# Delta-rule heads: the q/k norm of the next head ahead of this head's output, the second weight unit split in two steps, a new order in the prologue

## The chip, the cores and the metric

The kernel runs on one core of one Trainium2 chip. A core has four engines that matter here and run side by side: PE (TensorE, matrix multiplies), DVE (VectorE), ACT (ScalarE) and POOL (GpSimd). SP issues the weight transfers. Each engine works through its own list of instructions in the order in which they are written; they meet only at semaphores. The metric is the device time of one execution in microseconds (us), as the median of several runs.

## What is computed

Three layers on a 256 x 2048 activation in float32: a first block and two hybrid attention layers. The change touches the gated delta-rule part of the first block only. Cut to what matters there:

```python
h = rmsnorm(x, norm1_w[l])
proj = h @ w_in[l]
u_pool, q, k, v, z, a, bt, xr, gr = jnp.split(proj, cuts, axis=-1)
...
y_gdn = gated_deltanet(q, k, v, z, a, bt, gdn_conv_w[l], gdn_a_log[l], gdn_dt_bias[l], gdn_norm_w[l])
...
def l2norm(t):
    return t * lax.rsqrt(jnp.sum(t * t, axis=-1, keepdims=True) + EPS)
```

Six heads of 128 columns (`GH`). For each, q, k and v go through a causal convolution of four taps and a silu, q and k through `l2norm`, and then through the gated delta rule in chunks of 64 tokens: decays from cumulated gates, the inverse of a triangular matrix, a state handed from chunk to chunk. The output is normalised and multiplied by silu(z).

## The kernel before

**Weights.** Every weight matrix arrives in units of 128 x 2048 floats in the four buffers of `raw`. A float32 product is made of three passes with rounded halves: ACT copies `raw` to `w_hi` (L161), DVE subtracts to get `w_lo` (L166), each in two parts of 768 and 1280 columns, and PE runs three matmuls a tile (L197 to L199 in this stage): `w_hi` with the high and the low half of the activation, `w_lo` with the high half. A unit is 16 tiles, so 48 matmuls.

**Two kinds of work on PE.** In the delta-rule stage PE mixes the small matmuls of a head (`mix` of the tensor block, its variable j) with the projection of the next head's q, k, v and z. The function `fill(n)` issues n pieces of two tiles (six matmuls) of that projection; a head holds 32 pieces, four units numbered (i, 0) to (i, 3). Piece 3 of each unit is the first that needs the second part of `w_lo`. So PE has always something to do between two small steps, as long as what the small step waits for is ready when the pieces ahead of it are done.

**One head on PE**, in order: the sum of squares of q and k (`qk_ss`, one matmul pair of 512 columns); two pieces; the gate rows (`grow`, from `gb`, into `m[2]`); two pieces; a wait for `k_t`, the normalised k (`k_normed`); the transposes of k and v and the products k·k and k·q (`kkq`); five pieces; a wait for `u1`, that is for `tu` written at the end of DVE's chain; then five levels of the inverse, the state steps, the output, and its norm, with 21 more pieces among them.

**One head on DVE and ACT.** Their `mix(j, side)` holds the steps of head j, and `side(k)` calls put the steps of the next head's projection, convolution and silu between them. The order of both is written out by hand; nothing else sets it. Five of the six heads are one rolled loop (`Fori(1, GH)`), the last is written out behind it with `pool_side`. At the start of head j, ACT makes the norm factor from `qk_ss` (Ln, then Exp into `rs`), splits unit (i, 1) as a whole, finishes the silu of z of the head before (`sigmoid(i - 1, 3)`), makes `expg` from `grow`, and then the exponential of `dec`. DVE makes `q_t` and `k_t` from `rs`, one step of that silu (`one_plus`), the two `w_lo` parts of unit (i, 1), then `dec` from `grow` (it also waits for `expg`), waits for ACT's exponential (`edec`), and goes on through `dd`, `aa`, `xm` to `tu` (`u1`). At the end of a head come the output `oy` (DVE), its product with silu(z) on POOL (`oz`), the copy of its high half to `mixed` (ACT, `mix_hi`), the low half (DVE, `mix_lo`), `take(i, 3)` (DVE, the scaled z of the next head out of PSUM) and `take_z(i)` (ACT).

**The prologue** projects head 0, computes the gates (`gate_logs`, `beta`, `sums`, `bexpg`, `egd`) in a chain of tiny DVE operations, splits unit (1, 0) and squares q and k of head 0 (`squares(0)` into `sq`).

## Time and profile before

| | us |
|---|---|
| median of 3 runs (3514.66 to 3526.53) | 3518.19 |
| the profiled execution, its own time | 3525.01 |
| its span | 3523.3 |
| PE busy | 3413.3 (97%) |
| DVE busy | 2160.6 (61%) |
| ACT busy | 1701.2 (48%) |
| granted TensorE clock, mean | 0.991 |

The delta-rule heads take the stretch from 55 to about 322 us of the span. How to read it: PE is the engine that nearly always works, so time is what PE does plus what PE waits. The rows in the section after the next show single instructions with their start, their busy time, and in brackets the idle time of that engine just before and what ended it.

### The profile page before, as it was taken

The page shows a single profiled execution, that of the slowest core. Times are in us where ns is not written, and L with a number is a line of the kernel's source. Part 1 is how long each engine was busy: PE and PEld are TensorE (multiplying, and loading weights), DVE is VectorE, ACT ScalarE, POOL GpSimd, SP SyncE. Part 2 cuts the span into 40 slices and gives each one's busy share as a digit, 9 for nine tenths or more (in the row PEclk, how much of TensorE's full clock was granted, in tenths as well). Part 3 has the DMA queues.
Part 4 walks back from the last instruction along what each step waited for, and adds up shares of the span by engine and source line. Part 5 has one row for each costly group of instructions (what it writes and reads, how often), then busy time and mean ns, then how long its engine had stood idle before and what let it go on. Part 6 is the DMA issues. An engine that isn't in the chain of part 4 may idle for free. (4 is left out here: it accounts for less than half of the span.)

```text
span 3523.3 us, 73388 instructions
## 1 busy us (share of the span) xinstructions
PE 3413.3 (97%) x28014; PEld 3336.7 (95%) x28014; DVE 2160.6 (61%) x3526; ACT 1701.2 (48%) x2776; POOL 182.6 (5%) x208
## 2 busy tenths in 40 slices
PE   7889699999999999999999999999999999999999
PEld 7888699999999998899999999999899999999999
DVE  6666556656656665667755565555567765566554
ACT  4443544434434454655544554444565554554443
POOL 1000010000000014000000000000000000000000
PEclk9999899999999999999999999999999999999999
DMA  4223355555555554334455445454334355445554
GB/s 176 95 95 111 114 181 178 189 191 179 188 189 182 181 190 166 132 144 155 146 179 203 169 163 184 181 191 176 135 144 155 137 180 200 174 151 180 189 191 167
DMA packets 90613, 584.18 MB, mean 166 GB/s; under 512 B 10481, under 2 KB 11121, under 8 KB 28401
## 3 DMA queue, kind: packets, MB, share of 16 engines
q1 hardware_dynamic: 88992, 577.60, 46.4%
q0 software_dynamic: 1488, 4.72, 0.4%
q8 instruction: 94, 1.54, 0.2%
q14 instruction: 39, 0.31, 0.0%
HBM read 580.19 MB, written 2.10 MB: 165 GB/s over the span
## 5 line engine op out<-in xcount | busy, mean ns | idle before, releaser
L185 PE MATMUL bank<-h,w_hi 128*128 128x256 f32 x5808 | 1658.9, 286 | 37.7 <-DVE w_lo L166 28.2
L166 DVE TENSOR_TENSOR w_lo<-raw,w_hi 128x768 fp32r<-128x768 f32 (+5 forms) x1202 | 1347.8, 1130 | 471.0 <-ACT w_hi L161 468.0
L186 PE MATMUL bank<-h,w_hi 128*128 128x256 f32 x5808 | 1628.1, 280 | 0.0
L187 PE MATMUL bank<-h,w_lo 128*128 128x256 f32 x5808 | 1623.4, 280 | 0.0
L161 ACT ACTIVATE w_hi<-raw 128x768 fp32r<-128x768 f32 (+5 forms) x1202 | 1106.0, 968 | 253.6 <-PE bank L187 232.1
L185 PEld LDWEIGHTS bank<-h,w_hi 128*128 128x128 f32 x5808 | 1096.4, 189 | 53.3 <-issue 26.1
L186 PEld LDWEIGHTS bank<-h,w_hi 128*128 128x128 f32 x5808 | 1097.6, 189 | 2.8 <-issue 1.4
L187 PEld LDWEIGHTS bank<-h,w_lo 128*128 128x128 f32 x5808 | 1096.9, 189 | 0.0
L185 PE MATMUL bank<-mixed,w_hi 128*128 128x256 f32 x2400 | 677.1, 282 | 25.3 <-DVE mixed L990 15.9
L186 PE MATMUL bank<-mixed,w_hi 128*128 128x256 f32 x2400 | 673.3, 281 | 0.0
L187 PE MATMUL bank<-mixed,w_lo 128*128 128x256 f32 x2400 | 671.3, 280 | 0.0
L185 PEld LDWEIGHTS bank<-mixed,w_hi 128*128 128x128 f32 x2400 | 453.8, 189 | 26.9 <-DVE mixed L990 16.3
L186 PEld LDWEIGHTS bank<-mixed,w_hi 128*128 128x128 f32 x2400 | 454.2, 189 | 0.2
L187 PEld LDWEIGHTS bank<-mixed,w_lo 128*128 128x128 f32 x2400 | 453.9, 189 | 0.0
L222 DVE TENSOR_TENSOR pre<-bank,rn 128x256 f32<-128x256 f32 x246 | 103.9, 422 | 127.2 <-PE bank L187 126.7
L1781 ACT ACTIVATE sgy<-sgy 128x256 f32<-128x256 f32 x64 | 26.7, 418 | 291.0 <-DVE sgy L222 291.0
L222 DVE TENSOR_TENSOR sgy<-bank,rn 128x256 f32<-128x256 f32 x96 | 40.8, 425 | 194.3 <-PE bank L187 194.3
L197 PE MATMUL bank<-h,w_hi 128*128 128x256 f32 x432 | 137.7, 319 | 0.0
L1627 ACT ACTIVATE sqx<-pre 128x256 f32<-128x256 f32 x80 | 32.4, 414 | 192.2 <-DVE pre L222 192.2
L198 PE MATMUL bank<-h,w_hi 128*128 128x256 f32 x432 | 122.3, 283 | 0.0
L199 PE MATMUL bank<-h,w_lo 128*128 128x256 f32 x432 | 122.0, 282 | 0.0
L1580 POOL TENSOR_TENSOR zs<-pre,sig 128x256 f32<-128x256 f32 x48 | 39.8, 834 | 1311.9 <-DVE oy L1915 856.1
(351 smaller groups left out, 2574.4 us busy)
## 6 DMA issues: line engine op xcount, KB each, us to landing
raw<-in_w SPq DMA_DIRECT2D x485, 1024.0 KB, 4.8
raw<-in_w_br SPq DMA_DIRECT2D x96, 512.0 KB, 4.3
raw<-in_w_uq SPq DMA_DIRECT2D x8, 768.0 KB, 4.2
raw<-in_w_ukv SPq DMA_DIRECT2D x8, 512.0 KB, 3.3
bias_t<-in_bias POOLq DMA_DIRECT2D x16, 192.0 KB, 3.2
x<-in_x SPq DMA_DIRECT2D x4, 512.0 KB, 8.5
raw<-in_w_kr SPq DMA_DIRECT2D x4, 512.0 KB, 3.2
out_x<-x SPq DMA_DIRECT2D x3, 512.0 KB, 7.6
```

Of the source, the lines that this page charges most:

```text
L161: act.activation(w_hi[:, b % 2, c], raw[:, b, c], ACT.Copy).then_inc(S["hi_done"], 1)
L166: dve.tensor_tensor(w_lo[:, b % 2, c], raw[:, b, c], w_hi[:, b % 2, c].bitcast(F32), ALU.subtract).then_inc(S["lo_done"], 1)
L185: pe.matmul(o, w_hi[:, b % 2, c], a_hi, start=start and k == t0, stop=False)
L186: pe.matmul(o, w_hi[:, b % 2, c], a_lo, start=False, stop=False)
L187: last = pe.matmul(o, w_lo[:, b % 2, c], a_hi, start=False, stop=stop and k == t0 + nt - 1)
L197: pe.matmul(o, w_hi[:, b % 2, c], a_hi, start=k == 0, stop=False)
L198: pe.matmul(o, w_hi[:, b % 2, c], a_lo, start=False, stop=False)
L199: last = pe.matmul(o, w_lo[:, b % 2, c], a_hi, start=False, stop=k == KT - 1)
L222: return dve.tensor_tensor(dst, src[:, 0:SEQ], rn[:, :], ALU.mult)
L1580: pool.tensor_tensor(zs[:, e, :], pre[:, 7 + e, :], sig[:, e, :], ALU.mult).then_inc(S["z_silu"], 1)
L1627: act.activation(sq[:, k, :], src, ACT.Square).then_inc(S["h_sq"], 1)
L1781: act.activation(sg[:, b // 2, :], sg[:, b // 2, :], ACT.Sigmoid).then_inc(S["gate_sig"], 1)
```

## The change

On ACT, the two steps that make the norm factor of head j+1 (`norm_factor(j + 1)`) move from the start of the next head to this head's end, between `side(3)` and the wait for `oz`; `expg` of head j+1 (`decay_rows(j + 1)`) moves behind the copy to `mixed` and ahead of `take_z`. On DVE, `q_t` and `k_t` of head j+1 (`qk_normed(j + 1)`) move ahead of the wait for `mix_hi`. The split of unit (i, 1) comes in two steps. ACT: first part ahead of the exponential of `dec`, second part behind it. DVE: `dec` first, then `one_plus` and the first part, and the second part behind `qdec`, after `u1`.

In the prologue, ACT squares q and k of head 0 and splits unit (1, 0) ahead of the convolution of v; DVE makes the gate columns between the two parts of unit (1, 0), and `q_t` and `k_t` of head 0 ahead of the last gate steps. PE waits once more, for `sums_sb`, ahead of the transposes of k. PE's order of instructions is the same.

```diff
+        def split_hi_part(act, n, b, k, cols=UNIT):
+            at_least(act, f"raw_full{b}", 16 * n + 16)
+            at_least(act, "unit_done", 4 * n + b - 1)
+            c = parts(cols)[k]
+            act.activation(w_hi[:, b % 2, c], raw[:, b, c], ACT.Copy).then_inc(S["hi_done"], 1)
...
                 def side(k):
-                    if k == 0:
-                        split_hi(act, i, 1)
+                    if k == "split":
+                        split_hi_part(act, i, 1, 0)
+                    elif k == 0:
+                        split_hi_part(act, i, 1, 1)
                         sigmoid(i - 1, 3)
...
-            def mix(j, side):
+            def norm_factor(j):
                 act.wait_ge(S["qk_ss"], j + 1)
...
-                side(0)
+
+            def decay_rows(j):
                 act.wait_ge(S["grow"], j + 1)
                 act.activation(expg[:, :], m[2][:, 0:SEQ], ACT.Exp).then_inc(S["expg"], 1)
+
+            def mix(j, side, more=True):
+                side("split")
                 act.wait_ge(S["dec"], 2 * j + 2)
                 act.activation(dec[:, :], dec[:, :], ACT.Exp).then_inc(S["edec"], 1)
+                side(0)
...
                 side(3)
+                if more:
+                    norm_factor(j + 1)
                 act.wait_ge(S["oz"], j + 1)
...
+                if more:
+                    decay_rows(j + 1)
                 side(4)
...
-            split_hi(act, 1, 0)
-            squares(0)
+                    squares(0)
+                    split_hi(act, 1, 0)
+            norm_factor(0)
+            decay_rows(0)
             take_z(0)
...
                     if k == 0:
                         one_plus(i - 1, 3)
-                        split_lo(dve, i, 1)
+                        split_lo_part(dve, i, 1, 0)
+                    elif k == "split":
+                        split_lo_part(dve, i, 1, 1)
...
-            def mix(j, side):
+            def qk_normed(j):
                 dve.wait_ge(S["qk_rs"], j + 1)
...
-                side(0)
+
+            def mix(j, side, more=True):
                 dve.wait_ge(S["grow"], j + 1)
...
                                       gcum[:, p, bass.ds(j, 1)], 0.0, ALU.subtract, ALU.min).then_inc(S["dec"], 1)
+                side(0)
                 dve.wait_ge(S["edec"], j + 1)
...
                 dve.tensor_tensor(qdec[:, :], q_t[:, :], expg[:, :], ALU.mult).then_inc(S["qdec"], 1)
+                side("split")
                 side(1)
...
                 side(13)
+                if more:
+                    qk_normed(j + 1)
                 dve.wait_ge(S["mix_hi"], j + 1)
...
-            split_lo(dve, 1, 0)
-            take(0, 3)
-
+            split_lo_part(dve, 1, 0, 0)
             dve.wait_ge(S["beta_e"], 1)
...
+            dve.wait_ge(S["gate_g"], 1)
+            gate_columns(0)
+            split_lo_part(dve, 1, 0, 1)
+            take(0, 3)
             dve.wait_ge(S["gate_sums"], 1)
             dve.tensor_copy(sums[:, :], m[1][:, 32:60]).then_inc(S["sums_sb"], 1)
+            qk_normed(0)
...
-            gate_columns(0)
...
                 pe.wait_ge(S["k_normed"], j + 1)
                 pe.wait_ge(S["silu"], 4 * j + 3)
+                pe.wait_ge(S["sums_sb"], 1)
```

DVE at the end of the loop's body and behind the branch; `COMPARE_AND_BRANCH` closes an iteration, and `k_t` is what PE waits for early in a head. Before:

```order
L874 ISA [waits mix_hi]
L874 REGISTER_ALU
L874 TENSOR_TENSOR mixed<-oy,mixed 128x256
L690 REGISTER_ALU
L222 TENSOR_TENSOR pre<-bank,rn 128x256 [waits silu,unit_done]
L947 REGISTER_ALU
L947 COMPARE_AND_BRANCH
L812 SCALAR_TENSOR_TENSOR q_t<-pre,rs 128x256 [waits qk_rs]
L813 TENSOR_TENSOR k_t<-pre,rs 128x256
L707 TENSOR_SCALAR sig<-sig 128x256 [waits silu_e]
L166 TENSOR_TENSOR w_lo<-raw,w_hi 128x768 [waits hi_done]
L166 TENSOR_TENSOR w_lo<-raw,w_hi 128x1280 [waits hi_done]
```

The same place of the changed kernel:

```order
L837 SCALAR_TENSOR_TENSOR q_t<-pre,rs 128x256 [waits qk_rs]
L838 TENSOR_TENSOR k_t<-pre,rs 128x256
L904 ISA [waits mix_hi]
L904 REGISTER_ALU
L904 TENSOR_TENSOR mixed<-oy,mixed 128x256
L711 REGISTER_ALU
L228 TENSOR_TENSOR pre<-bank,rn 128x256 [waits silu,unit_done]
L979 REGISTER_ALU
L979 COMPARE_AND_BRANCH
L845 TENSOR_SCALAR dec<-m,gcum 128x128 [waits expg,grow]
```

`q_t` and `k_t` now stand ahead of the branch and of the low half of the output, and `dec` is the first operation behind the branch.

ACT at the start of a head. Before:

```order
L508 ACTIVATE rs<-m,eps 128x512 [waits qk_ss]
L511 ACTIVATE rs<-rs 128x512 [waits qk_ln]
L161 ACTIVATE w_hi<-raw 128x768 [waits unit_done,raw_full1]
L161 ACTIVATE w_hi<-raw 128x1280
L448 ACTIVATE sig<-sig 128x256 [waits silu_1p]
L450 ACTIVATE sig<-sig 128x256 [waits silu_ln]
L514 ACTIVATE expg<-m 128x256 [waits grow]
L516 ACTIVATE dec<-dec 128x256 [waits dec]
```

The same place of the changed kernel:

```order
L167 ACTIVATE w_hi<-raw 128x768 [waits unit_done,raw_full1]
L530 ACTIVATE dec<-dec 128x256 [waits dec]
L167 ACTIVATE w_hi<-raw 128x1280 [waits unit_done,raw_full1]
L454 ACTIVATE sig<-sig 128x256 [waits silu_1p]
L456 ACTIVATE sig<-sig 128x256 [waits silu_ln]
```

The factor and `expg` are gone from here (they stand at the end of the head before), and one part of the split is left ahead of the exponential of `dec`.

## Rows read from the trace of the kernel before

**Rows 1.** The page's first section: busy time and share of each engine.
```profile
PE 3413.3 (97%) x28014; PEld 3336.7 (95%) x28014; DVE 2160.6 (61%) x3526; ACT 1701.2 (48%) x2776; POOL 182.6 (5%) x208
```

**Rows 2.** The waits of PE, whole span: total us, times, longest us.
```profile
PE m L1092 <- DVE k_t L813: 11.9, 5, 2.4
PE m L1120 <- ACT sq L471: 5.0, 5, 4.2
...
PE m L1092 <- DVE tu L836: 2.8, 3, 0.9
```

**Rows 3.** Timeline, PE, head 2: start, us, instruction, [idle before, what ended it].
```profile
143.30 1.12 PE L1120 MATMUL m<-sq,shared 128*128 128x512 f32 x2 [0.21 <-ACT sq L471]
...
146.10 0.61 PE L1127 MATMUL m<-shared,gb 128*128 128x128 f32 x4
...
150.50 0.41 PE L1092 MATMUL m<-shared,k_t 128*128 128x128 f32 x2 [2.38 <-DVE k_t L813]
...
156.47 0.44 PE L1092 MATMUL m<-shared,tu 128*128 128x128 f32 x2 [0.95 <-DVE tu L836]
```

**Rows 4.** Timeline, ACT, the same head.
```profile
144.28 0.42 ACT L450 ACTIVATE sig<-sig 128x256 f32<-128x256 f32 x1
...
147.81 0.42 ACT L461 ACTIVATE sig<-pre 128x256 f32<-128x256 f32 x1 [1.05 <-DVE pre L222]
148.13 0.67 ACT L508 ACTIVATE rs<-m,eps 128x512 f32<-128x512 f32 x1
148.83 0.63 ACT L511 ACTIVATE rs<-rs 128x512 f32<-128x512 f32 x1
```

**Rows 5.** Timeline, DVE, the same head.
```profile
147.36 0.42 DVE L222 TENSOR_TENSOR pre<-bank,rn 128x256 f32<-128x256 f32 x1
149.50 0.42 DVE L812 SCALAR_TENSOR_TENSOR q_t<-pre,rs 128x256 f32<-128x256 f32 x1 [1.72 <-ACT rs L511]
...
152.80 0.60 DVE L819 TENSOR_SCALAR dec<-m,gcum 128x128 f32<-128x128 f32 x2
153.89 0.43 DVE L823 TENSOR_TENSOR dd<-dec,masks 128x256 f32<-128x256 f32 x1 [0.48 <-ACT dec L516]
...
155.99 0.42 DVE L836 TENSOR_TENSOR tu<-shared,xm 128x256 f32<-128x256 f32 x1
```

**Rows 6.** Line L161, 40 to 330 us: duration ns min/median/max, starts, forms.
```profile
L161 ACT ACTIVATE w_hi<-raw x54: 826/1050/1262, 39.9 to 328.9; 128x768 fp32r<-128x768 f32 x27, 128x1280 fp32r<-128x1280 f32 x27
```

**Rows 7.** Timeline, PE, from the end of the prologue into head 0.
```profile
55.19 2.07 PE L1120 MATMUL m<-sq,shared 128*128 128x512 f32 x2 [4.20 <-ACT sq L471]
...
62.27 0.38 PE L1092 MATMUL m<-shared,k_t 128*128 128x128 f32 x2
...
67.11 0.38 PE L1092 MATMUL m<-shared,tu 128*128 128x128 f32 x2
```

**Rows 8.** Timeline, DVE, the same stretch.
```profile
51.45 0.29 DVE L707 TENSOR_SCALAR sig<-sig 128x256 f32<-128x256 f32 x1 [0.48 <-ACT sig L466]
53.40 0.96 DVE L166 TENSOR_TENSOR w_lo<-raw,w_hi 128x768 fp32r<-128x768 f32 x1 [1.66 <-ACT w_hi L161]
54.56 1.49 DVE L166 TENSOR_TENSOR w_lo<-raw,w_hi 128x1280 fp32r<-128x1280 f32 x1 [0.20 <-ACT w_hi L161]
...
57.74 0.29 DVE L712 TENSOR_SCALAR gb<-shared,gate_g 128x128 f32<-128x128 f32 x1 [0.30 <-ACT egd L560]
...
58.94 0.43 DVE L812 SCALAR_TENSOR_TENSOR q_t<-pre,rs 128x256 f32<-128x256 f32 x1 [0.32 <-ACT rs L511]
```

**Rows 9.** Timeline, PE, head 4.
```profile
232.69 1.12 PE L1120 MATMUL m<-sq,shared 128*128 128x512 f32 x2 [0.21 <-ACT sq L471]
...
246.35 0.38 PE L1092 MATMUL m<-shared,tu 128*128 128x128 f32 x2
```

**Rows 10.** Busy by engine in a stretch, then PE's granted clock, DMA share, GB/s.
```profile
241.00:244.00 3.00, 3.00 (x17) 3.00 (x17) 2.48 (x5) 1.92 (x8) 1.28 (x1) 0.54 0.24 38
```

**Rows 11.** The waits of POOL: a wait on its own queue between two layers.
```profile
POOL qk L1568 <- POOLq L83: 8.3, 1, 8.3
```

More of the change, by code:

```diff
@@ L277, in first_block @@
     sb, at_least = g["sb"], g["at_least"]
-    load_unit, split_hi, split_lo, split_lo_part, unit, unit_tiles, of = (
-        g[k] for k in ("load_unit", "split_hi", "split_lo", "split_lo_part", "unit", "unit_tiles", "of"))
+    load_unit, split_hi, split_hi_part, split_lo, split_lo_part, unit, unit_tiles, of = (
+        g[k] for k in ("load_unit", "split_hi", "split_hi_part", "split_lo", "split_lo_part", "unit", "unit_tiles", "of"))
     x, h, ident, ones, eps = (g[k] for k in ("x", "h", "ident", "ones", "eps"))
@@ L496, in pool_side @@
             def pool_side(k):
-                if k == 0:
-                    split_hi(act, B_POOL, 1)
+                if k == "split":
+                    split_hi_part(act, B_POOL, 1, 0)
+                elif k == 0:
+                    split_hi_part(act, B_POOL, 1, 1)
                     sigmoid(GH - 1, 3)
@@ L563, in _ @@
                 mix(i - 1, head_side(i))
-            mix(GH - 1, pool_side)
+            mix(GH - 1, pool_side, False)
             def gates(i):
@@ L784, in pool_side @@
                     one_plus(GH - 1, 3)
-                    split_lo(dve, B_POOL, 1)
+                    split_lo_part(dve, B_POOL, 1, 0)
+                elif k == "split":
+                    split_lo_part(dve, B_POOL, 1, 1)
                     dve.wait_ge(S["pads"], 2)
@@ L944, in _ @@
             dve.wait_ge(S["egd"], 1)
-            gate_columns(0)
             with dve.Fori(1, GH) as i:
                 mix(i - 1, head_side(i))
-            mix(GH - 1, pool_side)
+            mix(GH - 1, pool_side, False)
             def pooled():
```

## The prediction

> **What bounds the kernel now.** First the page's busy shares: PE works 97% of the span, DVE and ACT about half [rows 1]. So the time can fall only where PE waits, or where it runs slow. Next the waits of PE over the whole span: in the heads three of them stand out [rows 2]. PE waits for `k_t` once in each of the heads 1 to 5 (11.9 us together), for `sq` (5.0 us, of which 4.2 is one wait, at the start of head 0), and for `tu` in three heads (2.8 us). Together 19.7 us, which the change is aimed at; no other engine has to get faster for that, only earlier. Then the timelines of one ordinary head, where the cause is seen. PE is free at 150.50 − 2.38 = 148.12 but `k_t` is not there [rows 3], since DVE had waited 1.72 us for `rs`, and ACT began `rs` (L508) only behind `take_z` (L461), which hung on the head's output [rows 4, 5]. After that `tu` is 0.95 us late as well [rows 3].
>
> **Heads 1 to 3: `k_t`.** New place of the norm factor: ACT starts its last Exp of `side(3)` at 144.28; the next operation can start 0.32 behind, as L508 does behind L461 [rows 4], so at 144.60. The sum of squares (L1120) is done at 143.30 + 1.12 = 144.42 [rows 3], so nothing is waited for. Exp follows the Ln by 0.70 (148.13 to 148.83) and `q_t` follows that by 0.67 (148.83 to 149.50) [rows 4, 5]: `q_t` at 145.97. PE could start 1.00 behind `q_t` (149.50 to 150.50) [rows 3, 5]: 146.97. PE comes there at 148.12, so this has 1.15 us in hand and the whole 2.38 goes. What is pushed back? The copy to `mixed`, `take(i, 3)` and `take_z` stand behind the moved steps. The factor is done on ACT at 144.60 + 0.70 + 0.63 = 145.93 and `k_t` on DVE at some 0.8 behind 145.97 (two 0.42 us operations), 146.8; both before 147.36 where `take(i, 3)` ran, with 0.34 for the low half ahead of it. I take nothing for it; cover gone, it would cost its own 0.2 to 0.5. `expg` needs `grow`, done at 146.10 + 0.61 = 146.71 [rows 3], and ends at about 147.1, ahead of `take_z` at 147.81. Cost nothing.
>
> **Heads 1 to 3: `tu`.** What is late next is DVE's chain to `u1`. In the new order `dec` starts right behind `take(i, 3)`: 147.36 + 0.34 = 147.70, plus the loop's branch, which now lies on this path. ACT crosses the same kind of branch between L461 and L508, 0.32 apart with a 0.42 us operation between them [rows 4]: no cost is seen; I take 0.15. So `dec` at 147.85 and done at about 148.5. On ACT the first part of the split starts at 147.81 + 0.32 + 0.15 = 148.28 and takes 0.83 [rows 6]: 149.11. DVE subtracts from 149.15, 0.96 us [rows 8], so it is free at about 150.0; ACT's exponential of `dec`, 0.42 us behind 149.0, is done inside that. Then L823 at 150.0 and `tu` 2.10 behind (153.89 to 155.99) [rows 5]: 152.1, and PE could start 0.48 behind that (155.99 to 156.47) [rows 3, 5]: 152.6. PE itself needs 156.47 − 0.95 − 150.50 = 5.02 us from the transposes to there [rows 3], so it arrives at 148.12 + 5.02 = 153.14. That leaves 0.5 us in hand, and the 0.95 goes too. The second part, now behind `tu`, is done at 152.1 + 0.34 + 0.34 + 1.4 = 154.2. PE wants it at its eleventh piece, some 3.2 us behind 153.14 (an estimate: two pieces of 0.7 and six short matmuls of the levels), and DVE is free for the first level at 154.5, when it is wanted at 154.8 (an estimate, by the same spacing as before). Cost nothing, with 0.3 in hand. Sum per head: 2.38 + 0.95 = 3.33; three heads, **10.0 us**.
>
> **Heads 4 and 5.** Here the clock enters. In head 4 the granted clock is 0.54 in the 3 us from 241 [rows 10], that is near the lower level of 1.2 GHz, right behind that head's wait for `k_t` (2.4 like the others [rows 2]); the wait for `tu` is hidden under it. From the sum of squares to the use of `tu` PE took 246.35 − 232.69 = 13.66 us [rows 9]. With no wait and the full clock it is 148.12 − 143.30 = 4.82 plus 5.02 [rows 3], 9.84. So 3.8 us each; head 5 has the same picture. **7.6 us**, if the slow stretch goes with the wait.
>
> **Prologue and head 0.** PE is free at 55.19 − 4.20 = 50.99 [rows 7]. `squares(0)` now runs near 45, so this wait goes, but unit (1, 0) is next: DVE is free behind L707 at about 51.65, its first part (0.96) is ready at 52.6 [rows 8]. PE needs it once L1120 is issued, 0.95 later (4.82 less the 1.4, 0.8 and 1.65 of what follows it), at 51.9: a new wait of 0.7. Two pieces (1.4) to 54.07. The gate columns: beta behind the first part at 52.6, the columns behind beta's two tiny operations (an estimate: 0.45) at 53.05, four of them in 0.88 (57.74 to 58.94 less a wait of 0.32 [rows 8]), so 53.95. In time. Gate rows 0.8, two pieces 1.65: PE stands before `k_t` at 56.5. DVE: second part 1.4 from 53.9 (54.56 and 1.49 long, the next can start 0.08 sooner [rows 8]), `take(0, 3)` at 55.3, `sums` 0.1 to 0.2, `q_t` at 55.76, PE 1.00 later at 56.76, a wait of 0.2. Then 5.02 to `tu`: 61.8. DVE's chain there: `q_t` and `k_t`, three tiny gate steps and the wait for `egd` (an estimate: 0.9 in all), `dec` at 57.3, then as above `tu` in time for 61.6. Before, that matmul ran at 67.11 [rows 7]: **5.3 us**. Of this about 2.3 is not wait but speed, since from L1120 to the `k_t` matmul it took 62.27 − 55.19 = 7.08 [rows 7] against 4.82 in an ordinary head [rows 3]. PE's added wait for `sums_sb` is over by 55.8: nothing.
>
> **Sum.** 10.0 + 7.6 + 5.3 = 22.9 us. From the first level on, each head runs as before relative to PE; and behind the heads all hangs on the last head's end, so it is shifted, not stretched. Against the profiled execution's own 3525.01 that is 3502.1. It lay 6.8 above the median, so for the median of the runs: 3518.19 − 22.9 = **3495.3 us**.
>
> **A rule of the Trainium skill against this change.** The row says that the branch costs ACT nothing that can be seen [rows 4]; on DVE it lay under the 1.72 us wait [rows 5], so its price there is between 0 and 1.7. The page "Runtime: NRT & Kernel Launch" (section Instruction fetch mechanics) says that a taken branch whose target lies outside the two blocks held by the engine has to fetch it first. By the page the branch moved onto DVE's chain could stall; by the row it does not, and the sum goes by the row.
>
> **The rivals.**
> (a) The branch costs DVE or ACT up to 1.7 us on the path to `tu`, the end of what rows 5 allow. 0.5 is in hand, so up to 1.2 us is lost at up to five crossings, 6.0 us: 3501.3. For it: the chain has the least in hand. Against: ACT's row. 12%.
> (b) The slow clock stays, and comes once in each head. In head 4 it cost 13.66 against 9.84 + 2.4 = 12.2, so 1.4 us; six heads, 8.5 us: 3503.8. Against: it followed the long waits. 7%.
> (c) The change doesn't do what it says: `k_t` is early, but `tu` is no earlier than before, because the first part on ACT, `dec`, its exponential and `one_plus` make a longer ring than I see. Then PE waits at `tu` instead of at `k_t`, the heads gain nothing, and only the prologue stays: 3518.19 − 5.3 = 3512.9. Against: it needs 3.3 + 0.5 us of error in one chain. 8%.
> (d) Slower: the branch makes an engine fetch, and that costs what a wait on an engine's own queue cost between two layers, 8.3 us [rows 11]. Now it lies ahead of `dec`, and PE stands at `tu`: (8.3 − 0.5) x 5 = 39.0 lost, 22.9 won: 3534.3. It turns the sign from (22.9 / 5) + 0.5 = 5.1 us on. For it: the body's code is laid out anew, so the old bound of 1.7 needn't hold. Against: PE and ACT cross their branches unharmed. 3%.
>
> **How the numbers follow.** My forecast has 70%. About 0.3% (10.6 us) is what can be told from no change. Faster by more: the forecast, (a) and (b), 89%. Within: (c), 8%. Slower: (d), 3%. Range: downwards, the five waits of 0.2 for `sq` and three slow stretches behind the heads could shift and spare 1.0 + 3 x 1.4 = 5.2, and the lowest run before lay 3.5 below its median: 3487. Upwards, (a) and (b) and part of the 8.3 by which the highest run lay above: 3508. Left out are (c), (d) and a little of the edges.
>
> **What would show it.** Right: in the waits of PE the row for `k_t` falls from 11.9 to below 1, the 4.2 for `sq` to about 0.7 for `w_lo`, none for `tu`; the sums of squares of two heads lie 41.4 us apart (they were (232.69 − 143.30) / 2 = 44.7 [rows 3, 9]), clock 1.00 there; PE busy the same but for the slow stretches. Wrong: a wait for `tu` of 0.5 to 1.7 (a); a clock near 0.5 in heads without a long wait (b); the `tu` wait at about 3 (c); DVE idle ahead of `dec` with nothing that ends it (d). The forecast also fails if DVE isn't free for the first level, which shows as a wait for `xm`.

## The result, and the profile after

| | before | after |
|---|---|---|
| median of the runs, us | 3518.19 (3514.66 to 3526.53) | 3497.12 (3495.77 to 3497.91) |
| ratio, 95% interval | | 0.9933 [0.992, 0.9945] |
| the profiled execution, its own time | 3525.01 | 3495.77 |
| its span | 3523.3 | 3494.1 |
| first matmul of the next projection, behind all heads | 436.36 | 413.50 |

The changed kernel is 21.07 us faster by the medians (0.60%; the interval excludes "no change"); the forecast was 22.9. Line numbers have moved: the sum of squares is L1152 (it was L1120), the matmuls with `k_t` and `tu` are L1124 (L1092), a level of the inverse L1196 (L1163), `dec` L845 (L819), `w_lo` L172 (L166), `w_hi` L167 in this stage (L161).

The page's busy times of the changed kernel, to be read against [rows 1]:

```profile
PE 3401.6 (97%) x28014; PEld 3324.6 (95%) x28014; DVE 2161.7 (62%) x3526; ACT 1702.0 (49%) x2776; POOL 179.6 (5%) x208
```

The waits of PE over the whole span (engine, line, waited for: us in total, times, longest us), against [rows 2]:

```profile
PE bank L191 <- DVE w_lo L172: 28.2, 5, 10.9
...
PE m L1191 <- DVE tu L876: 2.6, 5, 0.5
...
PE m L1152 <- ACT sq L477: 0.8, 4, 0.2
...
PE bank L203 <- DVE w_lo L172: 0.7, 1, 0.7
...
PE m L1124 <- DVE tu L863: 0.3, 1, 0.3
```

The row for `k_t` (11.9 us) is gone, that for `sq` fell from 5.0 to 0.8 us, and of the one for the first `tu` (2.8) 0.3 is left, in head 0. The 0.7 for `w_lo` at L203 is the new wait in the prologue that the forecast named. The first row, 28.2 us for `w_lo`, stands in the kernel before with the same sum, and the row for L1191 (a later level of the inverse, 2.6 us) too; the change doesn't touch them.

Timeline of PE in the changed kernel (start, us busy, instruction, [idle before, what ended it]); the first four rows are the prologue and head 0, against [rows 7], the next four head 2, against [rows 3], then the start of head 3 and the first matmul behind all heads:

```profile
51.32 1.10 PE L1152 MATMUL m<-sq,shared 128*128 128x512 f32 x2
53.12 0.39 PE L203 MATMUL bank<-h,w_hi 128*128 128x256 f32 x1 [0.70 <-DVE w_lo L172]
57.32 0.41 PE L1124 MATMUL m<-shared,k_t 128*128 128x128 f32 x2
62.70 0.44 PE L1124 MATMUL m<-shared,tu 128*128 128x128 f32 x2 [0.35 <-DVE tu L863]
...
135.91 1.12 PE L1152 MATMUL m<-sq,shared 128*128 128x512 f32 x2 [0.21 <-ACT sq L477]
140.59 0.38 PE L1124 MATMUL m<-shared,k_t 128*128 128x128 f32 x2
145.51 0.44 PE L1124 MATMUL m<-shared,tu 128*128 128x128 f32 x2
147.92 0.71 PE L1196 MATMUL m<-xm,tu 128*128 128x128 f32 x4
...
177.30 1.12 PE L1152 MATMUL m<-sq,shared 128*128 128x512 f32 x2 [0.21 <-ACT sq L477]
...
413.50 0.58 PE L191 MATMUL bank<-mixed,w_hi 128*128 128x256 f32 x1 [15.90 <-DVE mixed L1022]
```

In head 2 nothing is left in brackets ahead of `k_t` and `tu`. From its sum of squares to that of head 3 it is 177.30 − 135.91 = 41.39 us; it was 44.7.

Where the time went, by the same landmarks of both traces (the sums of squares of heads 0, 1 and 5, and that first matmul):

| stretch | before | after | difference | forecast |
|---|---|---|---|---|
| up to head 1's sum of squares | 98.58 | 94.48 | −4.10 | −5.3 |
| heads 1 to 4 | 179.16 | 165.56 | −13.60 | −13.8 |
| head 5 to the first matmul behind the heads | 158.62 | 153.46 | −5.16 | −3.8 |
| together | 436.36 | 413.50 | −22.86 | −22.9 |

The two profiled spans are 29.2 us apart, though. The other 6.3 us arise in code that the change doesn't touch. From that matmul to the start of the next layer, a stretch that is mostly the feed-forward part of the first block, it is 913.42 us before (436.36 to 1349.78) and 906.62 after (413.50 to 1320.12), 6.8 less; behind it 0.5 is lost again. Windows of 600 us there, before and then after (us, then busy time and count of PE, PEld, DVE, ACT, POOL, granted clock, DMA share, GB/s):

```profile
600.00:1200.00 600.00, 600.00 (x5097) 600.00 (x5096) 369.34 (x468) 257.64 (x325) 0.00 (x0) 1.00 0.54 186
```

```profile
600.00:1200.00 600.00, 600.00 (x5145) 600.00 (x5145) 371.90 (x472) 259.67 (x328) 0.00 (x0) 1.00 0.55 188
```

PE is never idle and the clock is 1.00 in both, yet one issues 5097 matmuls in the time in which the other issues 5145: 0.1177 against 0.1166 us apart. Whether the change did that had to be found out as well.

### The profile page after: what moved, and what is told of

Read it like the earlier page. It is cut to its first block and busy times, and to the rows that moved or that the text cites. A ratio compares the mean times of both kernels' runs of the same rounds, so it can differ in the third digit from the quotient of the medians.

```text
span 3494.1 us, 73390 instructions
## 1 busy us (share of the span) xinstructions
PE 3401.6 (97%) x28014; PEld 3324.6 (95%) x28014; DVE 2161.7 (62%) x3526; ACT 1702.0 (49%) x2776; POOL 179.6 (5%) x208
## 5 line engine op out<-in xcount | busy, mean ns | idle before, releaser
L191 PE MATMUL bank<-h,w_hi 128*128 128x256 f32 x5808 | 1655.2, 285 | 37.4 <-DVE w_lo L172 28.2
L172 DVE TENSOR_TENSOR w_lo<-raw,w_hi 128x768 fp32r<-128x768 f32 (+5 forms) x1202 | 1347.9, 1131 | 471.6 <-ACT w_hi L161 466.9
L161 ACT ACTIVATE w_hi<-raw 128x768 fp32r<-128x768 f32 (+4 forms) x1190 | 1093.9, 967 | 250.3 <-PE bank L193 228.9
L228 DVE TENSOR_TENSOR pre<-bank,rn 128x256 f32<-128x256 f32 x246 | 103.9, 422 | 124.0 <-PE bank L193 121.0
L228 DVE TENSOR_TENSOR sgy<-bank,rn 128x256 f32<-128x256 f32 x96 | 40.8, 425 | 195.2 <-PE bank L193 195.2
L203 PE MATMUL bank<-h,w_hi 128*128 128x256 f32 x432 | 135.0, 313 | 0.7 <-DVE w_lo L172 0.7
```

The source lines that it names most:

```text
L161: act.activation(w_hi[:, b % 2, c], raw[:, b, c], ACT.Copy).then_inc(S["hi_done"], 1)
L172: dve.tensor_tensor(w_lo[:, b % 2, c], raw[:, b, c], w_hi[:, b % 2, c].bitcast(F32), ALU.subtract).then_inc(S["lo_done"], 1)
L191: pe.matmul(o, w_hi[:, b % 2, c], a_hi, start=start and k == t0, stop=False)
L203: pe.matmul(o, w_hi[:, b % 2, c], a_hi, start=k == 0, stop=False)
L228: return dve.tensor_tensor(dst, src[:, 0:SEQ], rn[:, :], ALU.mult)
```

## The experiments

All kernels but the copies are edits of the changed kernel, and each computes the whole reference. "Period" is the distance between the sums of squares of two heads on PE in the profiled execution. In each group the kernel before ran beside: 3518.16 us in the first (heads_only to pool_later), 3517.28 in the second (to after_copy), 3524.46 in the third.

**heads_only: the old prologue with the new heads.**

```diff
-                    squares(0)
-                    split_hi(act, 1, 0)
-            norm_factor(0)
-            decay_rows(0)
+            split_hi(act, 1, 0)
+            squares(0)
             take_z(0)
...
+            norm_factor(0)
+            decay_rows(0)
...
             with act.Fori(1, GH) as i:
...
-            split_lo_part(dve, 1, 0, 0)
+            split_lo(dve, 1, 0)
+            take(0, 3)
...
-            gate_columns(0)
-            split_lo_part(dve, 1, 0, 1)
-            take(0, 3)
...
-            qk_normed(0)
...
+            gate_columns(0)
+            qk_normed(0)
...
             with dve.Fori(1, GH) as i:
```

Only PE's additional wait for `sums_sb` stays.

> The loop's new order (norm factor, expg, q_t and k_t of the next head at this head's end, unit (i, 1) in two steps) with the prologue as before. Theory A (the steps are additive, each priced from its own wait): heads 1 to 5 gain 17.6 us by the forecast's terms (10.0 + 7.6), so 3500.6; the wait of 4.2 us for sq and the slow clock behind it stay. By the trace of the changed kernel 17.4 to 17.9 us were won from the sum of squares of head 1 to the end of the heads. Rival B (part of the heads' gain came from entering them sooner or with a full clock): clearly less than 16 us.

Measured: 3501.64 us (3499.07 to 3510.41), ratio 0.9949 [0.9934, 0.9965]; periods 43.77 (head 0), then 41.42, 41.39, 41.40, 41.31. The wait of PE for `sq` is back:

```profile
PE m L1151 <- ACT sq L477: 5.0, 5, 4.2
```

The heads bring 16.5 us of the 21 by the medians. By the landmarks it is 320.9 us from head 1's sum of squares to the first matmul behind the heads, against 337.8 before and 319.0 in the changed kernel: 16.9 won of 18.8. The periods are those of the changed kernel, so the heads' gain does not come from the new prologue; the missing 1.9 lies behind head 5's sum of squares (155.39 us to the landmark, 153.46 in the changed kernel), where this kernel has a slow stretch of the clock and the changed one has none (more on it below). Head 1's sum of squares comes at 99.79, 1.2 later than before and 5.3 later than in the changed kernel. So the parts add up only roughly, and the new prologue by itself was not tried.

**norm_only: the norm moved, the split left whole ahead of `dec`.** The edit undoes the second half of the change:

```diff
                 side("split")
+                side(0)
                 act.wait_ge(S["dec"], 2 * j + 2)
                 act.activation(dec[:, :], dec[:, :], ACT.Exp).then_inc(S["edec"], 1)
-                side(0)
...
             def mix(j, side, more=True):
+                side(0)
+                side("split")
                 dve.wait_ge(S["grow"], j + 1)
...
-                side(0)
                 dve.wait_ge(S["edec"], j + 1)
...
-                side("split")
                 side(1)
```

> The changed kernel with the split of unit (i, 1) undivided and ahead of dec, as before; the norm factor, expg, q_t and k_t stay moved. Theory A (two chains in a row: behind k_t stands DVE's chain to tu): the wait for k_t stays gone, but PE then waits 2.2 us for tu in each head: the last part of the split is there at about 150.3 in the frame of the old head 2, dec at 151.7, tu 154.9, PE 155.4 against 153.1. Six heads, 13 us slower than the changed kernel, about 3510, so the moved norm alone is worth little. Rival B (the norm alone brings the gain, the split is decoration): within 2 us of the changed kernel, 3497.

Measured: 3514.27 us (3511.45 to 3525.96), ratio 0.9988 [0.9978, 0.9999]; 3510 was expected, with a wait of 2.2 us. PE's timeline in head 1, then its wait in all six heads:

```profile
98.21 1.12 PE L1152 MATMUL m<-sq,shared 128*128 128x512 f32 x2 [0.21 <-ACT sq L477]
102.88 0.38 PE L1124 MATMUL m<-shared,k_t 128*128 128x128 f32 x2
110.28 0.69 PE L1124 MATMUL m<-shared,tu 128*128 128x128 f32 x2 [2.41 <-DVE tu L864]
```

```profile
PE m L1124 <- DVE tu L864: 14.3, 6, 2.4
```

`k_t` comes without a wait, and PE stands 2.4 us at `tu` instead. The pair of matmuls behind that wait takes 0.69 us here, against 0.44 in the changed kernel: the clock had fallen. The stretches behind the wait in heads 1 and 2:

```profile
108.00:118.00 10.00, 7.64 (x52) 7.43 (x53) 5.87 (x13) 3.88 (x9) 0.00 (x0) 0.83 0.23 94
151.00:161.00 10.00, 7.56 (x63) 7.14 (x62) 6.67 (x16) 4.65 (x11) 1.13 (x1) 1.00 0.30 105
```

Head 1 has a granted clock of 0.83 in its 10 us, so a stretch at the lower level (1.2 GHz) lies in it, and head 2 has 1.00, with the same wait in both. The periods answer: 44.88 in head 1, 43.55 in head 2, then 45.00 and 43.48. A slow stretch costs 1.3 to 1.5 us here, and the same wait brings it in one head and not in the next. The expectation had left these stretches out; it missed by 4 us.

**split_only: the split in two steps, the norm back at the head's start.**

```diff
             def mix(j, side, more=True):
+                norm_factor(j)
+                decay_rows(j)
                 side("split")
...
-                if more:
-                    norm_factor(j + 1)
...
-                if more:
-                    decay_rows(j + 1)
...
-            norm_factor(0)
-            decay_rows(0)
...
             def mix(j, side, more=True):
+                qk_normed(j)
                 dve.wait_ge(S["grow"], j + 1)
...
-                if more:
-                    qk_normed(j + 1)
...
-            qk_normed(0)
```

> The changed kernel with norm factor, expg, q_t and k_t back at the start of the head; the split in two steps and the rest of the new prologue stay. Theory A: the wait for k_t is back, 2.4 us in each of five heads, none for tu: 12 us slower than the changed kernel plus 1.4 us for each slow stretch of the clock that follows such a wait (two before), about 3509 to 3512. Theory A also says of the clock: the slow stretches in the heads come back with the waits, in some heads, not in all. Rival C (the clock in the heads has nothing to do with these waits): 1.00 throughout the heads, as in the changed kernel.

Measured: 3516.01 us (3508.55 to 3520.18), ratio 0.9987 [0.9977, 0.9998], 4 us above what was expected (3509 to 3512). PE's wait in all heads, and the row of head 2:

```profile
PE m L1118 <- DVE k_t L834: 14.0, 6, 2.4
```

```profile
147.98 0.66 PE L1118 MATMUL m<-shared,k_t 128*128 128x128 f32 x2 [2.38 <-DVE k_t L834]
```

Now the wait for `k_t` is what it was [rows 3], in head 0 as well, and none is left for `tu`. Periods 45.15, 45.00, 43.53, 45.02 for heads 1 to 4: 43.53 in the head without a slow stretch. So in a head without a slow stretch each half alone brings some 1.2 us (44.70 to about 43.5) and both together 3.3; in a head with one the clock takes more than the 1.2 back (44.88 to 45.15). From head 1's sum of squares to the first matmul behind the heads norm_only won 1.5 us on the kernel before, split_only 1.9, and the two together 18.8. By the medians each half alone, with the new prologue, is 0.1% faster than the kernel before; that the gain comes from their being together is what these two show.

**pool_later: POOL's silu(z) multiplication kept behind DVE's first level of the inverse.** Looking for what had eaten the half microsecond that the forecast had in hand ahead of `tu`, I found one operation longer than before. All instances of the line in the kernel before, then in the changed kernel (duration ns min/median/max, first and last start, forms):

```profile
L833 DVE TENSOR_TENSOR xm<-aa,masks x6: 424/424/426, 65.0 to 290.1; 128x256 f32<-128x256 f32 x6
```

```profile
L860 DVE TENSOR_TENSOR xm<-aa,masks x6: 774/782/849, 61.3 to 268.3; 128x256 f32<-128x256 f32 x6
```

What lies beside it in head 2 of the changed kernel, DVE and then POOL:

```profile
144.22 0.78 DVE L860 TENSOR_TENSOR xm<-aa,masks 128x256 f32<-128x256 f32 x1
145.04 0.42 DVE L863 TENSOR_TENSOR tu<-shared,xm 128x256 f32<-128x256 f32 x1
```

```profile
143.99 0.74 POOL L401 TENSOR_TENSOR zs<-pre,sig 128x256 f32<-128x256 f32 x1 [5.16 <-ACT sig L456]
```

Before, that POOL multiplication began inside the second of two `w_lo` subtractions (128x1280; the profile merges both in one row, and the second starts at 151.4), and was itself the longer one. DVE, then POOL:

```profile
150.37 2.51 DVE L166 TENSOR_TENSOR w_lo<-raw,w_hi 128x768 fp32r<-128x768 f32 x2
```

```profile
152.19 1.29 POOL L395 TENSOR_TENSOR zs<-pre,sig 128x256 f32<-128x256 f32 x1 [5.99 <-ACT sig L450]
```

The edit makes POOL wait for the end of the first level of the same head (the semaphore `tu`, which counts the levels; the edit for head 0 is alike):

```diff
...
                 pool.wait_ge(S["oz"], i)
+                pool.wait_ge(S["tu"], 5 * i + 1)
                 silu(i, 3)
```

> The changed kernel, but POOL makes silu(z) of a head only once DVE has done its first level (a wait for tu). In the changed kernel xm (L860) took 0.78 us instead of 0.42 while POOL's multiplication ran, and tu came 0.36 later than worked out; the first level of the inverse stood 0.24 us further from the transposes than before. Theory D (POOL and DVE get in each other's way when both work on SBUF): L860 is back at 0.42 us, tu is ready 0.36 sooner in each head, and the 0.24 to 0.3 us goes: 1.4 to 1.8 us over six heads, 3495.5. Rival E (xm is slow for another reason, such as a late wait for aa): L860 stays at about 0.8 us and nothing moves.

Measured: 3493.57 us (3492.18 to 3503.34), ratio 0.9933 [0.9917, 0.9949]; periods 41.06, 41.03, 41.04, 40.95. The line has its old length again; the second fence is PE in head 1, from the sum of squares to the use of `tu`, 9.49 us:

```profile
L863 DVE TENSOR_TENSOR xm<-aa,masks x6: 424/424/426, 61.0 to 266.1; 128x256 f32<-128x256 f32 x6
```

```profile
93.76 1.12 PE L1155 MATMUL m<-sq,shared 128*128 128x512 f32 x2 [0.21 <-ACT sq L480]
...
103.25 0.39 PE L1127 MATMUL m<-shared,tu 128*128 128x128 f32 x2
```

DVE's 0.36 us came back as 0.37 us a head on PE, so that operation stood on the path: in head 2 the use of `tu` came 0.1 us sooner behind the sum of squares, and the first level 0.27 sooner behind `tu`. The longer `xm` follows from the overlap with POOL, since it went with it. In both kernels the operation that had started first kept its length and the other was longer: before, the subtraction (1.49 us, as long as in [rows 8]), and in the changed kernel POOL's (0.74, begun at 143.99, ahead of `xm` at 144.22). The page "SBUF — State Buffer" of the Trainium skill (section SBUF: two separate sides) says that the two engines share a pair of ports as an exclusive lock, which a DVE operation with two SBUF inputs and a GpSimd operation that reads SBUF take from each other. Both operations here are of that kind, and the trace agrees on who is delayed. In size it agrees only roughly: blocked until POOL's end at 144.73, `xm` with its 0.42 would have ended at 145.15, and it ended at 145.00.

By the landmarks less of this is left. At head 5's sum of squares pool_later is 2.2 us ahead of the changed kernel (257.84 against 260.04), at the first matmul behind the heads 0.75 (412.75 against 413.50). Between them lies the end of the last head, where PE waits 2.5 us for `w_lo` in both kernels. The same 10 us there, in the changed kernel and then in pool_later:

```profile
300.00:310.00 10.00, 7.50 (x65) 7.32 (x64) 8.46 (x16) 2.47 (x4) 1.31 (x2) 1.00 0.37 131
```

```profile
300.00:310.00 10.00, 7.50 (x52) 7.32 (x51) 7.91 (x16) 3.82 (x5) 0.00 (x0) 0.83 0.27 81
```

The granted clock is 1.00 in one and 0.83 in the other. The three executions of the changed kernel that were profiled, and chain_longer, have no slow stretch at this wait; heads_only, pool_later, pool_later2, chain_longer5, dve_unrolled and combined have one. What decides it stays open.

**chain_longer and chain_longer5: is anything in hand ahead of `tu`?** The first adds three copies (`tensor_copy` of `rn`) ahead of `dec` on DVE, the second five multiplications:

```diff
             def mix(j, side, more=True):
+                for k in range(5):
+                    dve.tensor_tensor(scratch[:, k, :], rn[:, :], rn[:, :], ALU.mult)
                 dve.wait_ge(S["grow"], j + 1)
```

> The changed kernel with three more copies (128x256, some 0.34 us each from start to start, 1.0 us in all) on DVE ahead of dec in each head. The forecast's theory (0.5 us in hand ahead of tu, so a branch or any other delay costs only what lies above that): 0.5 us a head, 3 us over six, 3500. Theory F (nothing is left in hand, since tu is now what PE starts on at once): 1.0 us a head, 6 us over six, 3503, and a wait of PE for tu of 1.0 in each head. Either way the k_t wait stays gone.

Measured: 3497.36 us (3496.14 to 3502.51), ratio 0.9935 [0.9913, 0.9956]; periods 41.43, 41.40, 41.40, 41.32, as in the changed kernel. A miss by both theories, and a weak experiment: three copies took far less than three multiplications do.

```profile
141.03 0.69 DVE L843 COPY scratch<-rn 128x256 f32<-128x256 f32 x3
```

> The changed kernel with five more multiplications (128x256, 0.34 us each, 1.7 us) on DVE ahead of dec in each head. The three copies of the run before took only 0.6 us and vanished: 0.2 of them beside the branch, 0.4 in the wait for w_hi. By that reading the chain has 0.2 + 0.4 in hand ahead of w_lo and nothing behind it: 1.7 - 0.6 = 1.1 us later tu, and a head period of 42.5. If PE too had something in hand (0.5 by the forecast): 42.0.

Measured: 3512.37 us (one run); periods 42.50, 42.45, 42.44, 42.37. DVE and PE in head 2:

```profile
144.02 1.76 DVE L843 TENSOR_TENSOR scratch<-rn 128x256 f32<-128x256 f32 x5
145.69 0.60 DVE L848 TENSOR_SCALAR dec<-m,gcum 128x128 f32<-128x128 f32 x2
```

```profile
150.27 0.44 PE L1127 MATMUL m<-shared,tu 128*128 128x128 f32 x2 [0.99 <-DVE tu L866]
```

The 1.67 us (144.02 to 145.69) cost 1.05 a head. The rest was taken up in two places, both seen in the changed kernel's DVE in head 2:

```profile
139.03 0.41 DVE L838 TENSOR_TENSOR k_t<-pre,rs 128x256 f32<-128x256 f32 x1
139.64 0.43 DVE L904 TENSOR_TENSOR mixed<-oy,mixed 128x256 f32 x1 [0.20 <-ACT mixed L553]
139.98 0.42 DVE L228 TENSOR_TENSOR pre<-bank,rn 128x256 f32<-128x256 f32 x1
140.50 0.61 DVE L845 TENSOR_SCALAR dec<-m,gcum 128x128 f32<-128x128 f32 x2
...
141.71 0.96 DVE L172 TENSOR_TENSOR w_lo<-raw,w_hi 128x768 fp32r<-128x768 f32 x1 [0.40 <-ACT w_hi L167]
142.58 0.42 DVE L850 TENSOR_TENSOR dd<-dec,masks 128x256 f32<-128x256 f32 x1
```

`dec` starts 0.52 behind the operation ahead of it (0.34 is the usual distance), and `w_lo` waits 0.40 for ACT's first part. Behind `w_lo` nothing absorbs anything. So there is slack on DVE ahead of the first part of the split, about 0.6 us, which is why the three copies cost nothing, and none between it and `tu`: what sets `tu` is ACT's first part, and then DVE.

**dve_unrolled: the branch on DVE taken away.** DVE's five heads are written out.

```diff
-            with dve.Fori(1, GH) as i:
+            for i in range(1, GH):
                 mix(i - 1, head_side(i))
```

> The changed kernel with DVE's loop over five heads written out, so that DVE crosses no branch. Rival (a) of the forecast in small (the branch lies on the path to tu): take to dec goes from 0.52 us to 0.34, tu is 0.18 us sooner, and heads 1 to 5 are 0.2 us shorter each (41.2 instead of 41.4). Theory G (the branch is hidden, the 0.52 is the waits for grow and expg): 0.52 and 41.4 stay.

Measured: 3501.9 us (one run); periods 41.10, 41.10, 41.07, 41.02, so 0.3 less a head. DVE in head 2:

```profile
137.71 0.41 DVE L838 TENSOR_TENSOR k_t<-pre,rs 128x256 f32<-128x256 f32 x1
138.09 0.42 DVE L904 TENSOR_TENSOR mixed<-oy,mixed 128x256 fp32r<-128x256 f32 x1
138.44 0.42 DVE L228 TENSOR_TENSOR pre<-bank,rn 128x256 f32<-128x256 f32 x1
138.77 0.60 DVE L845 TENSOR_SCALAR dec<-m,gcum 128x128 f32<-128x128 f32 x2
...
140.16 0.96 DVE L172 TENSOR_TENSOR w_lo<-raw,w_hi 128x768 fp32r<-128x768 f32 x1 [0.53 <-ACT w_hi L167]
```

Read against the rows of the changed kernel just above, this says which part of the loop costs. The branch lies between L228 and `dec`: 0.33 apart here, 0.52 there, so 0.19 for it. But that gain is lost at once: `w_lo` still waits for ACT, 0.53 now, and starts 1.72 behind L228, as it did (1.73). What came back is at L904, the low half to `mixed`: 0.38 behind `k_t` here, 0.61 there, and those 0.23 move everything behind it, `take` and ACT's part of the split too. That operation is addressed by the loop's variable, which a loop written out doesn't need: in the listing of the changed kernel above a REGISTER_ALU stands between its wait and the operation. That this is the reason is argued, not shown. Where the other 0.07 of the 0.3 lies was not traced. The single time says nothing against the 0.3 a head: this execution had the slower pace of the 600 us window (5097 matmuls). So Theory G failed, and rival (a) had the price of the branch right, but the gain comes from another place.

**before_copy, after_copy and after_beside: whose is the pace?** The kernels before and after, unchanged, once more, beside others on the same chip.

> The kernel before, unchanged. In the profiled execution of before PE's matmuls in the first feed-forward part stood 0.1177 us apart up to 1350 us of the span, in that of the changed kernel 0.1167, which alone makes 7 us of the difference of the two spans. Theory H (that pace belongs to the execution, not to the kernel): it can be 0.1167 here too, and with it the time is about 3515. Rival I (the pace hangs on the stretches of slow clock in the heads, which before has and the changed kernel hasn't): 0.1177 again.

> The changed kernel, unchanged, beside the others on one chip: 3497 as before, head periods of 41.4 us. Theory H (pace of matmuls in the first feed-forward part belongs to the execution): either 0.1167 or 0.1177. Rival I (no slow clock in the heads, so no slow pace): 0.1167 again.

> The changed kernel beside the others: head period 41.4 us, the time to compare the other two with (3492 to 3497 so far).

Measured: before_copy 3519.4 us (one run), periods 44.73, 44.71, 44.70, 44.62; after_copy 3492.4 (3491.98 to 3492.74), ratio 0.9918 [0.9898, 0.9937]; after_beside 3501.02 (3496.0 to 3507.94), ratio 0.9933 [0.9918, 0.9948], with periods 41.43, 41.38, 41.40, 41.32 as ever. The same window of before_copy and then of after_beside:

```profile
600.00:1200.00 600.00, 600.00 (x5146) 600.00 (x5145) 371.85 (x472) 259.61 (x328) 0.00 (x0) 1.00 0.55 188
```

```profile
600.00:1200.00 600.00, 600.00 (x5097) 600.00 (x5096) 369.33 (x468) 256.93 (x323) 0.00 (x0) 1.00 0.55 185
```

Here it is the kernel before that has the quick pace and the changed one that has the slow one. In before_copy the stretch from the landmark to the next layer takes 906.62 us (436.73 to 1343.35), as in the changed kernel. So the pace belongs to the execution and not to the change, and so do the 6.3 us. It also isn't the slow clock in the heads that brings it: before_copy has that clock and the quick pace. What sets it stays open. The heads differ between executions too: head 4 of before_copy has a granted clock of 1.00 and a period of 44.62, where head 4 of the first profile of the same kernel had the slow stretch of [rows 10] and 45.05.

**pool_later2 and combined: do the two gains add?** The first is the kernel of pool_later again, the second has the same wait on POOL and the five heads of DVE and ACT written out (the edits shown above, on ACT as on DVE).

> The changed kernel with POOL's silu(z) behind DVE's first level, again, now beside the changed kernel on one chip. Head period 41.03, 2.2 us below the changed kernel in the heads (6 x 0.36), so about 2 us in the time.

> The changed kernel with POOL's silu(z) behind DVE's first level, and the head loops of DVE and ACT written out. By the looks so far the head period is 41.4 us in the changed kernel, 41.03 with POOL later, 41.1 with DVE written out. If the two gains add (both shorten the one chain to tu and to the first level), the period is 40.7 to 40.8 and the time 3.5 to 4 us below the changed kernel; if PE's own work is the floor once tu is early (rival), the period is 41.0 and the time 2 us below.

Measured, in one group with after_beside (3501.02): pool_later2 3495.03 us (3494.3 to 3501.7), ratio 0.9922 [0.9909, 0.9935], periods 41.07, 41.04, 41.03, 40.96; combined 3497.58 (3494.54 to 3502.03), ratio 0.9925 [0.9912, 0.9938], periods 40.89, 40.88, 40.88, 40.81. By the periods the two gains, 0.37 and 0.3, give 0.52 together, which lies between the two expectations; ACT's loop is written out here too, which was not tried by itself. What ended them is seen on DVE of combined in head 2, where the first level now waits for PE:

```profile
145.12 0.42 DVE L875 TENSOR_TENSOR xm<-m,masks 128x256 f32<-128x256 f32 x1 [0.23 <-PE m L1194]
```

By the landmarks combined stands at the first matmul behind the heads at 411.98, against 413.50 in the changed kernel; at head 5's sum of squares it was 3.5 us ahead (256.58 against 260.04), and the slow stretch behind it took the rest. Its median shows no gain over pool_later2: 1 or 2 us are less than the scatter of the unchanged rest, in which one and the same kernel has lain from 3491.98 to 3507.94. Against the changed kernel in its own group, pool_later was 3.6 us lower (3493.57 against 3497.12 in another group) and pool_later2 6.0 lower; the intervals of the ratios overlap, so only its periods show that it is faster, not its time.

## Why the prediction was right, point by point

- **What bounds the kernel** was read rightly. The three waits of PE that the forecast named fell from 19.7 us to 1.1, with a new one of 0.7 in head 0, without any engine being faster: DVE and ACT are as busy as before.
- **Heads 1 to 3**, forecast 3.33 each: 3.29, 3.31 and 3.28 measured (periods 41.43, 41.39 and 41.41 against 44.72, 44.70 and 44.69). The order of the steps came as worked out: in the frame of the forecast `dec` stands at 147.89 (140.50 + 143.30 − 135.91) where 147.85 was written. The 0.15 for DVE's branch was 0.18 to 0.19, though it turned out to lie beside a wait for ACT.
- **"0.5 us in hand" ahead of `tu`** failed. There is nothing in hand: chain_longer5 lost all that reached behind `w_lo`. The step at fault is the one that put `tu` "2.10 behind" the first operation on `dec`. It took the distance from [rows 5], where POOL was elsewhere; with POOL's multiplication beside it the distance is 2.46 (142.58 to 145.04). The forecast never asked what POOL would lie beside. The other 0.35 went on PE's side: PE can be there 9.49 behind the sum of squares (pool_later, head 1, where nothing holds it), not 9.84. Both parts were too long, 4.82 for 4.65 to the matmuls with `k_t` and 5.02 for 4.84 from there. The forecast had let PE go on at the start of each wait, which is the end of the last matmul. Without a wait the next one starts ahead of that end: the last matmul ahead of `k_t` starts at 147.84 and is 0.27 long, and such matmuls start 0.12 apart, so PE would have gone on at 147.96 and not at 148.12. So 0.36 and 0.35 came off the 0.5, and PE came some 0.1 late (9.60 behind), too little for a row among the waits.
- **The first level, "0.3 in hand"**, failed too: PE gets from `tu` to the level's matmuls in 2.41 us (145.51 to 147.92) instead of 2.17. DVE comes late to it: `tu` was 0.3 later than forecast, then came `qdec`, the second part of the split and the next `take`, and only then the level, without a pause. In pool_later, where `tu` is in time, it is 2.14 to 2.19. Against that PE used `tu` 9.60 behind the sum of squares (145.51 − 135.91), where 9.84 was forecast. The two misses of 0.24 cancel, and that is luck: the forecast had 41.4 for the period as PE's own work without a wait, and PE's own work is no more than 41.03 (pool_later), the rest being delays that it had said would not come.
- **Heads 4 and 5**, forecast 3.8 each: the slow stretch of the clock went with the waits, and from 92 to 300 us the granted clock is 1.00. Head 4 gave 3.72, but its slow stretch belongs to the profiled execution: against before_copy, where that head has none, it is 3.29. Head 5 and what follows gave 5.16; the extra 1.4 fits a slow stretch near 330 us of the kernel before that the changed one doesn't have there, at the price that norm_only shows for one. The forecast had kept this for its range, not for its sum. It is luck as well: six of the edited kernels have that stretch again.

```profile
92.00:300.00 208.00, 199.78 (x1576) 187.12 (x1575) 144.08 (x284) 99.55 (x193) 16.70 (x23) 1.00 0.29 101
```

- **Prologue and head 0**, forecast 5.3: 4.1 measured, the largest miss of a term. The wait for `w_lo` was 0.70 as written and the one for `k_t` didn't come; but the sum of squares started at 51.32 and not at 50.99, `k_t` was used at 57.32 and not at 56.76, and `tu` had a wait of 0.35, at 62.70 and not at 61.8. The last 0.3 went at the first level, as in every head. The 0.33 at the start is no more than executions differ: in after_copy and after_beside the sum of squares starts at 51.53 and 51.01. What remains, 0.9 between the sum of squares and the first level, is `tu` (0.35 of waiting) and that level (0.3), and 0.2 on the way to `k_t` that no wait row shows.
- **The rivals.** (a), a branch on the path to `tu`, did not come: 0.19 us on DVE, absorbed, where up to 1.7 was allowed. The rolled loop does cost 0.3 us a head, but 0.23 of it at the low half to `mixed`, a place that the forecast took at nothing. (b), the slow clock in each head, did not come. It was not far off, though: in norm_only and split_only 2.4 us of waiting a head bring it back in four and in three of the six heads, at 1.3 to 1.6 us each. (c), a wait at `tu` in place of the one at `k_t`, is what norm_only does, and there it costs 2.4 us a head; with the split in two it fell. (d), a fetch of 8.3 us at the branch, did not come in any of the crossings. As for the rule of the Trainium skill on branches ("Runtime: NRT & Kernel Launch", section Instruction fetch mechanics), no run here shows a fetch there, and 0.19 us is all that the branch on DVE shows.
- **The total** is right partly by balance, and so by luck: 1.2 too much for the prologue, 1.4 too little behind the heads. The medians carry the scatter of the unchanged rest: they are 21.07 us apart here, 24.9 in the group of after_copy (3517.28 and 3492.4) and 23.4 in that of after_beside (3524.46 and 3501.02), with 22.9 in their midst. The profiled execution was forecast at 3502.1 and took 3495.77, 6.3 less, since it had the quick pace and that of the kernel before the slow one.

## What to carry to other kernels

Where two chains end late one behind the other, to shorten one moves the wait to the next: at the first matmul behind the heads norm_only stood 1.9 us and split_only 4.8 us ahead of the kernel before (434.49 and 431.53 against 436.36), the whole change 22.9, all three with the new prologue. When work is moved, ask what every other engine will then run beside it, those off the path too: a multiplication on POOL that delayed nobody before came to lie beside the tightest operation of DVE. And measure a small edit by landmarks inside the trace, since the unchanged rest of a long kernel can scatter by more than the edit is worth; and look at the clock between the landmarks, since one slow stretch more or less moves them by 1 to 2 us.

## What the runs showed of the hardware

- A DVE multiplication of 128x256 floats took 0.42 us alone and 0.78 (up to 0.85) when a POOL multiplication of the same size had begun 0.2 us ahead of it; POOL's took 0.74 then, and 1.29 when it began inside a DVE subtraction of 128x1280.
- A stretch of matmuls without any wait, at a granted clock of 1.00, ran in two paces, 0.1177 and 0.1166 us apart, in executions of the same kernel. That is about 6 us of this kernel's time. Its cause stays open.
- The same wait of 2.4 us brought the lower clock level in one head and not in the next, and at one wait of 2.5 us behind the heads some kernels had it and others not. In the heads of the changed kernel, with no wait above 0.7 us, it never came; chain_longer5 had waits of 1.0 in heads 1 to 5 without it, and one of 1.83 in head 0 with it.
- On DVE the end of a rolled loop's body cost 0.19 us between two operations (0.52 against 0.33), and an operation of the same loop on `mixed` 0.23 more than in the loop written out.
- Three DVE copies of 128x256 floats took 0.69 us, five multiplications of that size 1.76: a copy some 0.2 each, a multiplication 0.35.
